# Attention bias products before the first norm's column sums, with their table and evictions on VectorE

## What is computed

```python
def rms_norm(x, gain, eps):
    x32 = x.astype(jnp.float32)
    y = x32 * lax.rsqrt(jnp.mean(x32 * x32, axis=-1, keepdims=True) + eps)
    return (y * gain.astype(jnp.float32)).astype(x.dtype)
...
        bucket = t5_bucket(k_pos[None, :] - q_pos[:, None])
        bias = rel_bias[bucket].astype(jnp.float32).transpose(2, 0, 1)
...
        p = jax.nn.softmax(logits + bias[None, :, None], axis=-1)
...
        h = rms_norm(x, pre_norm[l], NORM_EPS)
        proj = h @ w_in[l]
```

## Time and profile before

| what | us |
|---|---|
| median of 3 runs | 2353.24 |
| lowest and highest | 2352.44 and 2355.54 |
| the profiled execution's own time | 2360.57 |
| its span | 2358.5 |
| TensorE busy | 2217.1 (94%) |
| VectorE busy | 1297.5 (55%) |
| ScalarE busy | 876.5 (37%) |
| GpSimd busy | 611.7 (26%) |

### The profile page before, as it was taken

How to read it: one execution, slowest core, us unless ns; L and a number is a source line. 1 busy time by engine, 2 the same in 40 slices (tenths; PEclk the granted TensorE clock), 3 DMA queues, 4 the chain that set the end, 5 groups by cost and what they waited for, 6 DMA issues and landing times.

```text
span 2358.5 us, 24729 instructions
## 1 busy us (share of the span) xinstructions
PE 2217.1 (94%) x9408; PEld 1545.3 (66%) x9408; DVE 1297.5 (55%) x1894; ACT 876.5 (37%) x1372; POOL 611.7 (26%) x282
## 2 busy tenths in 40 slices
PE   8999999988999999979989999999899899999997
PEld 4677765665777755656758775665467588756654
DVE  5687844546787744456598623332255985233322
ACT  4432354334422353333553313442145533133421
POOL 3333330334233321334332100113143221001130
PEclk8999999998999999998989998999899899989998
DMA  5322321422323321332220012122322200211221
GB/s 206 106 75 96 108 72 45 143 81 71 120 64 99 103 63 54 116 107 67 83 63 28 19 54 63 41 61 94 123 72 74 63 28 19 63 55 45 80 81 54
DMA packets 48012, 180.20 MB, mean 76 GB/s; under 512 B 5522, under 2 KB 6418, under 8 KB 46488
## 3 DMA queue, kind: packets, MB, share of 16 engines
q1 hardware_dynamic: 47800, 178.49, 23.9%
q10 hardware_dynamic: 96, 0.13, 0.0%
HBM read 163.92 MB, written 14.68 MB: 76 GB/s over the span
## 4 chain that ended last, share of the span: by engine, by line
PE 72%; DVE 22%; ACT 3%; issue 2%; DMA 0%; DVEq 0%; ACTq 0%
PE bank L554 12%; PE bank L563 12%; PE bank L568 11%; PE bank L626 4%; PE bank L767 4%; PE bank L1000 4%; PE bank L960 2%; PE bank L638 2%; PE bank L974 2%; PE bank L959 1%; PE bank L645 1%; PE bank L780 1%; DVE arena L1506 1%; PE bank L706 1%; PE bank L577 1%
## 5 line engine op out<-in xcount | busy, mean ns | idle before, releaser
L2071 POOL TENSOR_TENSOR w_lo<-wraw,w_hi 128x1024 fp32r<-128x1024 f32 (+1 forms) x206 | 508.0, 2467 | 1530.4 <-ACT w_hi L1022 1530.4
L1022 ACT ACTIVATE w_hi<-wraw 128x1024 fp32r<-128x1024 f32 (+1 forms) x206 | 216.6, 1051 | 748.2 <-PE bank L568 408.4
L554 PE MATMUL bank<-h_hi,w_hi 128*128 128x512 f32 x1648 | 456.1, 418 | 38.1 <-ACT h_hi L1034 30.3
L554 PEld LDWEIGHTS bank<-h_hi,w_hi 128*128 128x128 f32 x1648 | 312.1, 193 | 170.2 <-issue 83.7
L563 PE MATMUL bank<-h_lo,w_hi 128*128 128x512 f32 x1648 | 410.9, 392 | 0.0
L568 PE MATMUL bank<-h_hi,w_lo 128*128 128x512 f32 x1584 | 391.4, 389 | 0.0
L563 PEld LDWEIGHTS bank<-h_lo,w_hi 128*128 128x128 f32 x1648 | 311.4, 189 | 68.6 <-POOL h_lo L2067 0.3
L568 PEld LDWEIGHTS bank<-h_hi,w_lo 128*128 128x128 f32 x1584 | 296.1, 187 | 63.1
L626 PE MATMUL bank<-arena,wdir 128*128 128x512 f32 x256 | 114.3, 598 | 0.0
L1988 DVE TENSOR_TENSOR bank<-bank,con 128x128 f32<-128x128 f32 x64 | 19.2, 299 | 172.3 <-PE bank L960 171.4
L1000 PE MATMUL bank<-arena,wdir 128*128 128x512 f32 x256 | 112.4, 592 | 0.0
(11 more groups left out here) (317 smaller groups left out, 3089.9 us busy)
## 6 DMA issues: line engine op xcount, KB each, us to landing
wraw<-in_w_split SPq DMA_DIRECT2D x204, 512.0 KB, 3.6
wdir<-in_w_direct SPq DMA_DIRECT2D x60, 512.0 KB, 3.6
x_park<-arena SPq DMA_DIRECT2D x3, 2048.0 KB, 6.3
arena<-x_park SPq DMA_DIRECT2D x3, 2048.0 KB, 7.8
hg_park<-arena SPq DMA_DIRECT2D x2, 2048.0 KB, 9.5
arena<-hg_park SPq DMA_DIRECT2D x2, 2048.0 KB, 8.4
arena<-bias_rows SPq DMA_DIRECT2D x2, 1792.0 KB, 7.5
arena<-in_xT SPq DMA_DIRECT2D x2, 1024.0 KB, 7.0
```

The costliest lines, as they stand in the source:

```text
L554: mm(ps[0:wd, 0:S], hi[:, k, :].bitcast(F32R), h_hi[:, k, :].bitcast(F32R), start=k == 0 and not begun, stop=False)
L1022: a(w_hi[:, n % 2, 0:f].bitcast(F32R), wraw[:, n % 2, 0:f], ACT.Copy).then_inc(hi_done, 1)
L2071: nc.gpsimd.tensor_tensor(w_lo[:, n % 2, 0:f].bitcast(F32R), wraw[:, n % 2, 0:f], w_hi[:, n % 2, 0:f], ALU.subtract).then_inc(lo_done, 1)
```

## The change

The 8 bias products, their bank reader and the table that feeds them are placed differently:

- in `psum_plan()` the 8 bias jobs come first and the column-sum job ninth. The bias jobs so have banks 0 to 7, and the column sums take bank 0 after its first bias row is evicted;
- TensorE issues the 8 bias products ahead of the 8 column products. It waits for the bias loads and the table first, and for the constants only behind the column products;
- ScalarE no longer evicts the bias banks. VectorE does, with 8 `tensor_copy` from PSUM to `wide`, ahead of the first reciprocal;
- VectorE fills the `relw` table once the 2 bias loads have landed. Its wait for the 5 constant loads stands behind the evictions.

```diff
--- before.py
+++ after.py
@@ -98,7 +98,7 @@
 
 def psum_plan():
 
-    jobs = [("ss", "A0")] + [("bias", h, half) for h in range(H) for half in range(2)]
+    jobs = [("bias", h, half) for h in range(H) for half in range(2)] + [("ss", "A0")]
 
     def transform(kind, l, o):
         return [(kind, l, o, n) for n in range(8)]
@@ -578,8 +578,6 @@
                 ins.then_inc(filled(*job), 1)
 
             pe.wait_ge(*after("ones"))
-            column_sums(("ss", "A0"), [(hs["A0"][:, k, :], ("sq", "A0", k)) for k in range(KT)])
-            pe.wait_ge(const_in, 16 * NCONST)
             pe.wait_ge(bias_in, 32)
             for h in range(H):
                 for half in range(2):
@@ -587,6 +585,8 @@
                     ps = take(*job)
                     pe.wait_ge(*after("relb", h))
                     mm(ps[:, :], relw[:, h, :], onehot[:, half * 512:half * 512 + 512], start=True, stop=True).then_inc(filled(*job), 1)
+            column_sums(("ss", "A0"), [(hs["A0"][:, k, :], ("sq", "A0", k)) for k in range(KT)])
+            pe.wait_ge(const_in, 16 * NCONST)
 
 
             for l in range(DEPTH):
@@ -1051,10 +1051,6 @@
             squares("A0", lambda k: (x_first[k // 4], 16))
             root(("ss", "A0"), D, EPS6)
             split_weights(0)
-            for h in range(H):
-                for half in range(2):
-                    act.wait_ge(*full("bias", h, half))
-                    a(wide[:, h, half * 512:half * 512 + 512], bank("bias", h, half)[:, :], ACT.Copy).then_inc(release("bias", h, half), 1)
             split_weights(1)
             act.wait_ge(const_in, 16 * NCONST)
             a(sel[:, :].bitcast(F32R), sel_raw, ACT.Copy).then_inc(up("sel"), 1)
@@ -1473,11 +1469,15 @@
                 link(v.memset(small[:, n:n + 1], val))
             v.memset(relw[:, :, :], 0.0).then_inc(up("ones",), 1)
             dve.wait_ge(*after("ones",))
-            dve.wait_ge(const_in, 16 * NCONST)
             dve.wait_ge(bias_in, 32)
             for h in range(H):
                 v.tensor_scalar(relw[:, h, :], relw[:, h, :], relb[:, h:h + 1], None, ALU.add).then_inc(up("relb", h), 1)
                 dve.wait_ge(*after("relb", h))
+            for h in range(H):
+                for half in range(2):
+                    dve.wait_ge(*full("bias", h, half))
+                    v.tensor_copy(wide[:, h, half * 512:half * 512 + 512], bank("bias", h, half)[:, :]).then_inc(release("bias", h, half), 1)
+            dve.wait_ge(const_in, 16 * NCONST)
 
             def recip():
                 link(v.reciprocal(rs[:, :], rs[:, :]))
```

## The result

| | median, us | runs |
|---|---|---|
| kernel before | 2354.39 (2352.44 to 2355.96) | 4 |
| changed kernel | 2370.55 (2368.64 to 2371.45) | 4 |
| changed by before | 1.0068, 95% interval 1.0051 to 1.0085 | |

The change makes the kernel slower by 0.7%: 16 us, with 12 to 20 inside the interval. The forecast was 2364.1 with a range of 2357.0 to 2368.5, so the direction was right and the measured time lies 2 us above the range.

The account below looks back on a forecast made before the run. The last-ending chain lay 72% on TensorE and 22% on VectorE. Bias products, column sums and root to u_1 put u_1 at 52.45 instead of 41.55; 10.9 on the median 2353.24 gave 2364.1, range 2357.0 to 2368.5.

Parts of the forecast that it names:

- Start of the bias products: TensorE at program start: relb lands at 6.8, table steps take 1.20, first bias product at about 7.3 instead of 18.83.
- Their length at 1.2 GHz throughout: Bias products on TensorE: 32-row passes stay at the low clock, 16 x 0.853 = 13.65 us, from 7.3 to 21.0.
- Rival A: Bias products on TensorE lift the clock as any busy stretch does: u_1 at 45.6, +4.1, 2357.3 us; chance 0.10.
- Rival C: First passes on TensorE are long because of the first loads, not the idle clock: +0.3, 2353.5 us; chance 0.04.
- Column sums: TensorE behind the bias products: 7 long passes (5.97) and 9 short (3.84), 9.8 us, ending at 30.8 instead of 18.83.
- D: Column sums on TensorE stay at 1.2 GHz to the end, 34.7, adding 3.8: 2368.0 us; chance 0.05.
- Evictions cost nothing: VectorE's 8 copies from PSUM take about 0.7 each, 5.6 us in all, hidden while VectorE has nothing else until 32.9.
- Root to u_1: Chain from root at 32.2 to u_1's first product at 52.45: 18.67 as in phase A1, plus 1.6 for w_lo.
- u_1 moves by 10.9: First product of u_1, the second projection tile, on TensorE: at 52.45 instead of 41.55, 10.9 us later.
- From u_1 to the time: Rest of the kernel: what u_1 is late the end is late, 10.9 us on the median 2353.24, giving 2364.1.
- Rival B: Clock as forecast, but h and u_0 keep the pace of before: u_1 at 46.65, +5.1, 2358.3 us; chance 0.08.
- rival E: Table on VectorE doesn't start before the constants land (13.07): everything 6 us later, 2370 us; chance 0.02.

Follow-up runs that it names:

- the second profile: Changed kernel profiled again without any edit, to repeat it; median 2369.65 us, 1.0061 to the kernel before.
- experiment 4: Changed kernel with its 8 evictions back on ScalarE, between the squares and the root; 2369.0 us, 1.0060 to the kernel before.
- the repeat: Timed runs of both kernels again, no edit: changed kernel 2369.65 us, kernel before 2355.47; 14.3 us longer (11.3 to 17.2).

## Why the prediction was wrong

Step by step, forecast and measured in the profile of the changed kernel:

- **Start of the bias products**: forecast 7.3, measured 7.56. Right.
- **Their length at 1.2 GHz throughout**: 13.65, measured 13.99. Right, and for the reason given: with 128 rows they took 9.36. Rival A is out. Rival C, that the first loads slow the passes, is out too, as the column products still had long passes from 21.6 to 25.8 at a DMA share of 0.00. The prediction's own argument against C doesn't hold, though: beside u_0 has a DMA share of 0.61.
- **Column sums**: 9.8 and an end at 30.8; measured 9.19 and 30.74. The level did come up on the way, and D is out. That the end fits to 0.1 is luck: 5 long passes instead of 7 made up for a later start and longer bias products. In the second profile the sums took 9.82 and ended at 31.4.
- **Evictions cost nothing**: 0.69 each on VectorE, all in idle time. Right for the two orders compared. That ScalarE's would have hidden the root's table load (experiment 4) the prediction didn't see.
- **Root to u_1**: 20.27, measured 22.03. This is the term of the sum that failed: its mechanism was right and its size too small. Its first part, the second `w_lo` in the way of h, was put at 1.6 and measured 2.1. The prediction took one more tile at the long form of the earlier trace rows, which is a wait for an `h_lo` of half the size. The tile waits for the rest of a whole `w_lo`. The rule of the Trainium skill ("SBUF — State Buffer", "Who interferes with whom"), that the loser waits for the whole instruction, gave 2.35 as its upper bound, and the trace agrees better with it than with my pick: `w_lo` went on for 2.3 us from the start of h. The second part is the clock: 18.67 was taken from A1, where the last 16 passes of u_0 took 4.74 as the level came back in their middle. Here they took from 48.19 to 54.13, 5.94, because it came back at 53.0. Together 1.7 of the 1.76.
- **u_1 moves by 10.9**: measured 12.6 and 13.3. The mechanism was right and the size too small by about 2.
- **From u_1 to the time**: the forecast put its shift on a median of three runs, 2353.24. Over 15 to 29 runs it is 2356. Of the 6.4 us between the forecast, 2364.1, and the measured 2370.55 the baseline is thus 2.9, and the sum at u_1 is 1.7. The last 1.8 have no place in any profile. The difference in the first comparison was 16.2, where the repeat gave 14.3, so chance is the likely source, but that isn't shown.

So two things failed. In the sum it was the step from root to u_1; alone it would have put the forecast at 2365.9, inside the range. The other is the baseline with its range: the upper end allowed 4.4 us over the forecast for everything, from the sentence that took 3.1, the spread of three runs, for the spread of the kernel. Runs of the kernel before go from 2350.4 to 2360.9.

Rival B is out, as h took 10.61 and not 5.39, and rival E, as the table ran at 7.14.

## What to carry to other kernels

Before moving work ahead of a chain, look at what it covers where it stands: eleven microseconds on the chain of waits were worth nothing there, because root, reciprocal and scaling ran beside them, and in front of the chain they put it 11.9 us back. Then ask what the moved neighbours collide with: rounding the weight tiles sooner put GpSimd's `w_lo` beside VectorE just as h began. And take the baseline of a 0.5% question from twenty runs, not three.

## What the runs showed of the hardware

- Products over 32 rows at 100% busy neither held TensorE at 2.4 GHz nor brought it there: behind the column products it fell 2.8 us after they began, and at the start of the program 16 passes took 13.99, all of the long form, in four profiles. Padded with zeros to 128 rows the same products took 9.36 at the start and 6.9 to 7.0 behind other work. The Trainium skill ("TensorE: Matmul & The Clock Gate", Part 1) speaks of how busy the PE is; by that they should have got up. The measurement decides: padding with zeros made the products faster.
- One `w_lo` of 2.3 us on GpSimd held the scaling that began beside it, an instruction with two SBUF inputs: 2.87 instead of 0.75. The reciprocal, with one, took 3.35 beside a `w_lo` and without.
- The square root's table load stood behind the wait for the sums when the instruction ahead of it was a square, and ahead of that wait when a copy came between (16.76 against 30.80; 22.36 with the evictions). That is 1.4 us off the chain where the root is on it, for an order that costs nothing.
